# Later hybrid units and the memory stage of a two-block model: order of splits, copies and PSUM banks

## The chip, the cores and the metric

The kernel runs on one core of one Trainium2 chip, in one launch. The metric is the device time in microseconds of one execution. The core has a matrix engine (TensorE, "PE" in the profile, its weight loads "PEld"), a vector engine (VectorE, DVE), a scalar engine (ScalarE, ACT), GpSimd (POOL), and a queue engine (SyncE, SP) that here only issues DMAs.

## The reference, cut to what matters

256 tokens of width 1024 go through two models, each of two layers. A layer of the first model is a gated feed-forward part, a hybrid mixer, cross attention to 256 memory tokens, and a second feed-forward part. The change touches the last two thirds of the hybrid mixer and the cross attention, in both layers.

```python
for l in range(2):
    x = x + 0.5 * rms_norm(swiglu(rms_norm(x, g1), ...), p1)
    y = hybrid_mixer(rms_norm(x, g2), w_in[l], ...)       # attention with window and selection, + retention, then @ w_out
    x = x + rms_norm(y, p2)
    y = memory_xattn(rms_norm(x, g3), rms_norm(mem, gm), wq[l], wk[l], wv[l], wo[l])
    x = x + rms_norm(y, p3)
    x = x + 0.5 * rms_norm(swiglu(rms_norm(x, g4), ...), p4)

def memory_xattn(h, m, wq, wk, wv, wo):                   # 4 heads of 256
    q, k, v = h @ wq, m @ wk, m @ wv
    p = softmax(einsum('bthd,bmhd->bhtm', q, k) / 16)
    return einsum('bhtm,bmhd->bthd', p, v) @ wo
```

## The kernel before, in words

Everything stays on the chip; only weights are streamed. Twelve stages follow one another (`STAGES`): feed-forward, hybrid, memory, feed-forward for layer 0, the same for layer 1 (its hybrid stage begins 651.5 us after that of layer 0), then four stages of the second model. Each of the five engines has its own program, written out by hand in the order in which it runs; engines meet only at semaphores. `q.wait_ge(*act.at("memory", l, 7))` waits until ACT has done the instruction of that name. An engine runs its list in order, so whatever stands behind a wait waits too.

**Splits.** A product in full precision is made of three in a rounded format: each weight item of 128 x 2048 is split into a high part (ACT copies `raw` to `whi`, or to `mhi`) and a low part (DVE subtracts, giving `wlo` or `mlo`), in two halves of 128 x 1024. `take(s, tag, c, ahead)` brings both engines' splits up to that item plus `ahead` items. A split waits for the item's DMA (four `raw` buffers, loaded in order by SP when the item four places earlier is split) and for the last use of the home that it writes. In the second part of the hybrid stage three homes rotate. PE waits for the low part (`weights(i)`).

**Hybrid units.** `HUNITS` are eight units u = 0..7, four heads each; units 0 to 3 belong to the first 128 tokens (m = 0, one key block), units 4 to 7 to the second 128 (m = 1, two key blocks). For a unit, PE makes scores (256 columns of f32 for m = 1), DVE adds the bias and takes the maximum (`head(u)`), ACT makes the exponentials (`exps`), PE turns them (block k = 0 into bank 0, k = 1 into bank 1), ACT copies block 0 and, for m = 1, DVE copies block 1 to `hPT` (both named `h_pt`), PE multiplies with the values (`h_values`, bank 2), DVE scales them (`value`, with `weight` for the factors) and POOL adds them.

Between these, PE does work of the next stage, which needs nothing of the units: sixteen **memory pieces** p = 0..15, two in each unit. Pieces 0 to 7 make one tile of the memory keys each, pieces 8 to 15 the memory values, two pieces for one output. All of them write PSUM bank 3, and ACT copies bank 3 away (`memory_piece` in ACT's program); the next piece that starts an output waits for that copy. In unit u the order on PE is: scores(u+1), piece 2u, turns(u), piece 2u+1, values(u). On ACT: copy of piece 2u, h_pt(u), exps(u+1), copy of piece 2u+1, the split of `HSPLIT[u]` (wk2, wk3, wv0, wv1, wv2, wv3, w_out0, w_out1). On DVE: head(u+1), value(u-1), weight(u), h_pt(u) for m = 1, then the same split. `blocks`, `halves` and `fin` turn and split finished parts of the mixer's output for `w_out`: the retention part in unit 2, the first tokens' attention part in units 4 and 5.

**Memory stage.** After the queries (`wq`, heads 2 and 3 directly, 0 and 1 from the rows `QN`), PE makes for each head c scores, turns and outs, and then multiplies with `wo` (items wo0 and wo1, with more of the heads' work beside them, `beside_0` and `beside_1`, and then wo2 and wo3). DVE's `scores(c)` takes the maximum, waits for ACT's exponentials and scales them. DVE also scales two of the queries (`query(2, 2)`, `query(3, 3)`). PE before the change, from the second tile of wq3 on: scores(1), turn(0), scores(2), outs(0), turn(1), scores(3), wo0, outs(1), turn(2), turn(3), wo1, outs(2), outs(3), wo2 with wo3.

The matmul instruction of all products is L1653, that of all turns L1658; ACT's instruction is L690; DVE's are L1093 (two tensors), L1097 (tensor and scalars), L1101 (tensor, scalar, tensor), L1105 (copy), L1109 (maximum or sum).

Of the kernel before, what the change touches and what calls it, by code (L numbers as in the profile page):

```python
# [262 lines left out]
def build(nc, A, out):  # L263
    ctx = ExitStack()
    with ctx:
# [418 lines left out]
        def scalar(e):  # L684
# [154 lines left out]
            def memory_piece(s, p):  # L839
                l = STAGES[s][1]  # L840
                if p < 8:
                    q.wait_ge(*pe.at("memory", l, p))
                    if p >= 4:
                        q.wait_ge(*dve.at("ret_x", l, 1))
                    put(mkT[:, p * 256:(p + 1) * 256], PS[:, 3, 0:256], ACT.Copy, ("memory", l, p))
                    return
# [13 lines left out]
            def hybrid(s):  # L860
# [69 lines left out]
                for u, (m, g, br) in enumerate(HUNITS):  # L930
                    memory_piece(s, 2 * u)
                    q.wait_ge(*pe.at("h_turned", l, u, 0))
                    put(hPT[u % 2][:, 0:512], PS[:, 0, :], ACT.Copy, ("h_pt", l, u))
                    if u < 7:
                        exps("h", l, u + 1, 128 * (HUNITS[u + 1][0] + 1), hP, 0.125)
                    else:
                        take(s, *HSPLIT[u], 0)
# [6 lines left out]
                    if u == 5:  # L944
                        halves(s + 0.5, 0, 0, 0)
                    if u < 7:
# [12 lines left out]
            def memory(s):  # L959
# [29 lines left out]
                scores(0)  # L989
                scores(1)  # L990
                turned(0)
                scores(2)
                outs(0)
                turned(1)
                scores(3)

                def beside_0():
                    outs(1)
# [88 lines left out]
        def vector(e):  # L1087
# [235 lines left out]
            def hybrid(s):  # L1323
# [134 lines left out]
                head(0)  # L1458
                q.wait_ge(*pe.at("ret_out", l))
# [10 lines left out]
                for u, (m, g, br) in enumerate(HUNITS):  # L1470
                    if u < 7:
                        head(u + 1)
                    if u:
# [13 lines left out]
                    if m:  # L1487
                        q.wait_ge(*pe.at("h_turned", l, u, 1))
                        cp(hPT[u % 2][:, 512:1024], PS[:, 1, :], ("h_pt", l, u))
# [3 lines left out]
                    if u == 4:  # L1493
                        fin(s, l, 0)
                    if u == 5:
# [16 lines left out]
            def memory(s):  # L1512
                l = STAGES[s][1]

                def scores(c):
# [3 lines left out]
                    ts(nb[:, o:o + 2], mx[:, o:o + 2], -0.0625, None, ALU.mult, ALU.bypass, ("ms_max", l, c))  # L1519
                    q.wait_ge(*act.at("ms_exp", l, c, 1))  # L1520
# [16 lines left out]
                take(s, "wq", 3)  # L1537
                query(3, 3)
                scores(0)
                scores(1)  # L1540
                scores(2)
                outs(0)
                scores(3)
                take(s, "wo", 0)
                outs(1)
# [103 lines left out]
        def tensor(e):  # L1649
# [236 lines left out]
            def memory_piece(s, p):  # L1886
                l = STAGES[s][1]
                if p < 8:
# [3 lines left out]
                    if p:  # L1892
                        q.wait_ge(*act.at("memory", l, p - 1))
                    up_tile(hi, lo, f, 3, 0, mhv, mlv, ("memory", l, p), *([("used", i)] if f else []))
# [12 lines left out]
            def hybrid(s):  # L1907
# [134 lines left out]
                for u, (m, g, br) in enumerate(HUNITS):  # L2042
# [7 lines left out]
                    for k in range(m + 1):  # L2050
# [6 lines left out]
                        if u == 6 and k == 0:  # L2057
                            q.wait_ge(*dve.at("a", s + 0.5, 0, 0))
                        if u == 4 and k == 1:
                            q.wait_ge(*dve.at("a", s + 0.5, 1, 1))  # L2060
# [263 lines left out]
```

## Time and profile before

| | us |
|---|---|
| median of 3 runs | 1903.04 |
| lowest and highest of them | 1902.19, 1905.67 |
| the profiled execution's own time | 1902.21 |
| its span, first to last instruction | 1900.4 |
| PE busy | 1858.0 (98%) |
| DVE, ACT, POOL busy | 1317.2, 1042.3, 215.4 |
| granted TensorE clock over the span | 0.994 |

The profile is of one execution. Times in it are counted from the first instruction. A row of the timeline shows when a run of like instructions started and how long it lasted, and in brackets how long the engine had been idle before it and whose instruction ended that wait. The matmuls overlap in the pipe, so what a piece of PE's work costs is read from the starts of neighbouring rows rather than from their lengths. The granted clock is 1.00 where TensorE ran at 2.4 GHz and 0.50 where it ran at 1.2 GHz. All rows below are of layer 0 unless their group says otherwise.

### The profile page before, as it was taken

The numbers are of one execution on the slowest core, as the hardware profiler recorded it, in microseconds if no ns is written. First come the engines' busy times: TensorE is split into PE (matmuls) and PEld (weight loads), VectorE is DVE, ScalarE is ACT, GpSimd is POOL, SyncE is SP. The second block draws the span as 40 slices with busy tenths as digits, with TensorE's granted clock in tenths as the row PEclk, the third lists the DMA queues.
The fourth block names the chain that finished last, engine by engine and source line by source line (L and its number), as shares of the span: only waits on it lengthen the run. The fifth ranks groups of instructions, "written<-read, shape, count | busy, mean of one in ns | idle before, by whom it ended". The sixth has DMA issues, their size and how long they took to land.

```text
span 1900.4 us, 27884 instructions
## 1 busy us (share of the span) xinstructions
PE 1858.0 (98%) x10911; PEld 1617.2 (85%) x10911; DVE 1317.2 (69%) x1734; ACT 1042.3 (55%) x1503; POOL 215.4 (11%) x264
## 2 busy tenths in 40 slices
PE   6999999999999999999999999999999999999998
PEld 6888899788888888888997978888888888888887
DVE  5776758675766676667577667667787667787665
ACT  5555545555555555555465555555666445665453
POOL 1010102010100011001020101000301110301110
PEclk9999999999999999999999999999999999999999
DMA  8585654244565556766333626654636555635552
GB/s 297 184 298 190 165 179 134 89 159 163 173 217 182 180 189 216 268 169 214 121 129 111 204 96 213 201 185 158 211 104 221 179 199 164 219 111 195 193 188 79
DMA packets 229971, 339.46 MB, mean 179 GB/s; under 512 B 22278, under 2 KB 178064, under 8 KB 229840
## 3 DMA queue, kind: packets, MB, share of 16 engines
q1 hardware_dynamic: 221968, 307.91, 49.2%
q0 software_dynamic: 7872, 29.78, 4.8%
q8 instruction: 85, 1.39, 0.3%
q14 instruction: 46, 0.38, 0.1%
HBM read 336.62 MB, written 1.05 MB: 178 GB/s over the span
## 4 chain that ended last, share of the span: by engine, by line
PE 85%; DVE 11%; ACT 2%; issue 1%; DMA 1%; DVEq 0%; SPq 0%; ACTq 0%
PE ps L1653 82%; DVE wlo L1093 3%; PE ps L1658 3%; DVE xn L1093 2%; DVE region L1101 1%; ACT region L690 1%; DVE xs L1101 1%; DVE ahl L1093 1%; DVE mlo L1093 1%; DVE sm L1109 1%; ACT ahl L690 1%; DMA raw<-ffn_w_gate 1%; ACT whi L690 1%; DVE hlo L1093 0%; DVE region L1093 0%
## 5 line engine op out<-in xcount | busy, mean ns | idle before, releaser
L1093 DVE TENSOR_TENSOR wlo<-raw,whi 128x1024 fp32r<-128x1024 f32 (+2 forms) x458 | 561.8, 1227 | 184.8 <-ACT whi L690 150.2
L690 ACT ACTIVATE whi<-raw 128x1024 fp32r<-128x1024 f32 (+2 forms) x458 | 482.5, 1054 | 64.8 <-PE ps L1653 14.9
L1653 PE MATMUL ps<-ahl,whi 128*128 128x512 f32 (+1 forms) x1920 | 433.4, 353 | 0.3
L1653 PEld LDWEIGHTS ps<-ahl,whi 128*128 128x128 f32 x1920 | 331.2, 190 | 43.2 <-DVE hlo L1093 0.9
L690 ACT ACTIVATE region<-ps 128x512 f32<-128x512 f32 (+2 forms) x260 | 150.1, 577 | 326.6 <-PE ps L1653 248.8
L1653 PE MATMUL ps<-whi,ahl 128*128 128x512 f32 (+2 forms) x1120 | 303.6, 349 | 8.8 <-DVE ahl L1093 8.5
L1653 PE MATMUL ps<-ahl,wlo 128*128 128x256 f32 x1568 | 269.1, 282 | 0.0
L1653 PEld LDWEIGHTS ps<-ahl,wlo 128*128 128x128 f32 x1568 | 233.3, 191 | 11.9
L1653 PEld LDWEIGHTS ps<-whi,ahl 128*128 128x128 f32 x1120 | 198.0, 191 | 36.1 <-DVE ahl L1093 12.0
L1093 DVE TENSOR_TENSOR mlo<-raw,mhi 128x1024 fp32r<-128x1024 f32 x130 | 160.9, 1238 | 48.0 <-ACT mhi L690 38.0
L1653 PE MATMUL ps<-wlo,ahl 128*128 128x512 f32 (+2 forms) x560 | 191.6, 342 | 0.0
L1653 PE MATMUL ps<-whi,hhi 128*128 128x512 f32 x472 | 185.6, 393 | 1.1 <-DVE hlo L1093 1.1
L1653 PE MATMUL ps<-wlo,hhi 128*128 128x512 f32 x472 | 184.3, 391 | 0.0
L1653 PE MATMUL ps<-whi,hlo 128*128 128x512 f32 x472 | 183.7, 389 | 0.0
L531 POOL TENSOR_TENSOR hlo<-region,hhi 128x512 fp32r<-128x512 f32 x62 | 81.0, 1306 | 799.7 <-ACT hhi L690 799.7
L1653 PE MATMUL ps<-ahl,mhi 128*128 128x512 f32 (+1 forms) x640 | 144.5, 354 | 0.1
L1653 PE MATMUL ps<-region 128*128 128x64 f32 (+5 forms) x928 | 137.1, 335 | 7.2 <-DVE region L1105 7.1
L690 ACT ACTIVATE mhi<-raw 128x1024 fp32r<-128x1024 f32 x130 | 137.5, 1058 | 11.1 <-PE ps L1653 2.8
L1093 DVE TENSOR_TENSOR region<-region,ps 128x512 f32<-128x512 f32 x102 | 70.2, 688 | 95.4 <-ACT region L690 88.9
L1653 PEld LDWEIGHTS ps<-region 128*128 128x128 f32 (+2 forms) x928 | 113.2, 183 | 26.9 <-ACT region L690 9.7
L690 ACT ACTIVATE hhi<-region 128x512 fp32r<-128x512 f32 x68 | 43.0, 632 | 156.8 <-DVE region L1101 83.4
L1653 PEld LDWEIGHTS ps<-ahl,mhi 128*128 128x128 f32 x640 | 110.8, 190 | 14.6 <-DVE hlo L1093 0.3
(166 smaller groups left out, 2385.0 us busy)
## 6 DMA issues: line engine op xcount, KB each, us to landing
raw<-w_ff SPq DMA_DIRECT2D x64, 1024.0 KB, 5.4
raw<-ffn_w_gate SPq DMA_DIRECT2D x44, 1024.0 KB, 5.3
raw<-ffn_w_up SPq DMA_DIRECT2D x44, 1024.0 KB, 5.5
raw<-ffn_w_down SPq DMA_DIRECT2D x44, 1024.0 KB, 4.9
raw<-w_in SPq DMA_DIRECT2D x38, 1024.0 KB, 5.7
raw<-w_out SPq DMA_DIRECT2D x16, 1024.0 KB, 4.9
raw<-xa_wk SPq DMA_DIRECT2D x8, 1024.0 KB, 5.2
raw<-xa_wv SPq DMA_DIRECT2D x8, 1024.0 KB, 5.0
```

Source lines behind the costliest of these rows:

```text
L531: e.tensor_tensor(o, a, b, op).then_inc(*pool.did(*names))
L690: e.activation(o, i, f, **kw).then_inc(*act.did(*names))
L1093: e.tensor_tensor(o, a, b, op).then_inc(*dve.did(*names))
L1101: e.scalar_tensor_tensor(o, a, s, b, op0, op1).then_inc(*dve.did(*names))
L1109: e.tensor_reduce(o, a, AX.X, op).then_inc(*dve.did(*names))
L1653: m = e.matmul(o, l, r, start=start, stop=stop)
L1658: m = e.transpose(o, i, CS[0:k, 0:k])
```

## The change

It reorders four programs in the hybrid and memory stages and moves four tiles of each hybrid stage to another PSUM bank. No product is added or removed.

- ACT, units 3 to 6: the split of `HSPLIT[u]` stands ahead of exps(u+1); before, it stood at the unit's end. Unit 7 stays as it was.
- DVE, units 4 to 7: the copy h_pt(u) stands ahead of value(u-1) and weight(u). DVE also splits the first half of wk0 right after head(0).
- Memory pieces 1, 3, 5 and 7 write bank 1, and PE waits for the copy of piece p-2. In unit 2, `blocks` of the retention part stand behind values(2) and wait for the copy of piece 5.
- `fin(0)` moves on DVE from unit 4 to unit 5, and `blocks` and `halves` of the first tokens from unit 5 to unit 6 on PE, ACT and DVE.
- Memory stage: DVE's `scores(c)` is cut into `maximum(c)` and `normal(c)`; maximum(0) and normal(0) stand ahead of query(3). ACT's turned(0) stands ahead of exps(1), turned(1) ahead of exps(2), and outs(1) ahead of exps(3). PE's outs(1) stands ahead of wo0.

```diff
@@ -842,7 +842,7 @@
...
                         q.wait_ge(*dve.at("ret_x", l, 1))
-                    put(mkT[:, p * 256:(p + 1) * 256], PS[:, 3, 0:256], ACT.Copy, ("memory", l, p))
+                    put(mkT[:, p * 256:(p + 1) * 256], PS[:, (3, 1)[p % 2], 0:256], ACT.Copy, ("memory", l, p))
                     return
...
@@ -931,19 +931,19 @@
...
                     put(hPT[u % 2][:, 0:512], PS[:, 0, :], ACT.Copy, ("h_pt", l, u))
+                    if u >= 3:
+                        take(s, *HSPLIT[u], 0)
                     if u < 7:
                         exps("h", l, u + 1, 128 * (HUNITS[u + 1][0] + 1), hP, 0.125)
-                    else:
-                        take(s, *HSPLIT[u], 0)
                     memory_piece(s, 2 * u + 1)
...
                         fin(s, l, 0)
-                    if u == 5:
+                    if u == 6:
                         halves(s + 0.5, 0, 0, 0)
-                    if u < 7:
+                    if u < 3:
                         take(s, *HSPLIT[u], 0)
...
@@ -987,15 +987,15 @@
...
                 scores(0)
+                turned(0)
                 scores(1)
-                turned(0)
-                scores(2)
                 outs(0)
                 turned(1)
+                scores(2)
+                outs(1)
                 scores(3)
...
                 def beside_0():
-                    outs(1)
                     turned(2)
...
@@ -1456,6 +1456,7 @@
...
                 head(0)
+                split_to(number[s, "wk", 0], halves=1)
                 q.wait_ge(*pe.at("ret_out", l))
...
@@ -1470,6 +1471,9 @@
...
                         head(u + 1)
+                    if m:
+                        q.wait_ge(*pe.at("h_turned", l, u, 1))
+                        cp(hPT[u % 2][:, 512:1024], PS[:, 1, :], ("h_pt", l, u))
                     if u:
...
@@ -1484,15 +1488,12 @@
...
                     weight(u)
-                    if m:
-                        q.wait_ge(*pe.at("h_turned", l, u, 1))
-                        cp(hPT[u % 2][:, 512:1024], PS[:, 1, :], ("h_pt", l, u))
                     if u == 2:
...
                             halves(s + 0.5, h, 1, h)
-                    if u == 4:
+                    if u == 5:
                         fin(s, l, 0)
-                    if u == 5:
+                    if u == 6:
                         halves(s + 0.5, 0, 0, 0)
...
@@ -1512,11 +1513,14 @@
...
 
-                def scores(c):
+                def maximum(c):
                     o = 2 * (c % 2)
...
                     ts(nb[:, o:o + 2], mx[:, o:o + 2], -0.0625, None, ALU.mult, ALU.bypass, ("ms_max", l, c))
+
+                def normal(c):
+                    o = 2 * (c % 2)
                     q.wait_ge(*act.at("ms_exp", l, c, 1))
...
@@ -1535,14 +1539,18 @@
...
                 take(s, "wq", 3)
+                maximum(0)
+                normal(0)
                 query(3, 3)
-                scores(0)
-                scores(1)
-                scores(2)
+                maximum(1)
+                normal(1)
+                maximum(2)
                 outs(0)
-                scores(3)
+                normal(2)
+                maximum(3)
+                outs(1)
+                normal(3)
                 take(s, "wo", 0)
-                outs(1)
                 take(s, "wo", 1)
...
@@ -1889,9 +1897,11 @@
...
                     hi, lo = weights(i)
-                    if p:
-                        q.wait_ge(*act.at("memory", l, p - 1))
-                    up_tile(hi, lo, f, 3, 0, mhv, mlv, ("memory", l, p), *([("used", i)] if f else []))
+                    if p >= 2:
+                        q.wait_ge(*act.at("memory", l, p - 2))
+                    elif p:
+                        q.wait_ge(*dve.at("g_r", l, 1))
+                    up_tile(hi, lo, f, (3, 1)[f], 0, mhv, mlv, ("memory", l, p), *([("used", i)] if f else []))
                     return
...
@@ -2054,19 +2064,15 @@
...
                             q.wait_ge(*dve.at("h_pt", l, u - 1))
-                        if u == 6 and k == 0:
+                        if u == 7 and k == 0:
                             q.wait_ge(*dve.at("a", s + 0.5, 0, 0))
                         if u == 4 and k == 1:
-                            q.wait_ge(*dve.at("a", s + 0.5, 1, 1))
+                            q.wait_ge(*act.at("memory", l, 7))
                         for i in range(4):
...
                     q.wait_ge(*act.at("h_pt", l, u))
-                    if u == 2:
-                        for h in range(2):
-                            q.wait_ge(*dve.at("ret_x", l, h))
-                            blocks(s + 0.5, h, 1, h)
                     if m:
...
@@ -2076,7 +2082,12 @@
...
                                *([("h_values", l, u)] if (i, k) == (3, m) else []))
-                    if u == 5:
+                    if u == 2:
+                        q.wait_ge(*act.at("memory", l, 5))
+                        for h in range(2):
+                            q.wait_ge(*dve.at("ret_x", l, h))
+                            blocks(s + 0.5, h, 1, h)
+                    if u == 6:
                         q.wait_ge(*dve.at("fin", l, 0))
...
@@ -2139,9 +2150,9 @@
...
                 scores(3)
+                outs(1)
 
                 def beside_0():
-                    outs(1)
                     turn_scores(2)
...
```

## Rows read from the trace of the kernel before

**Rows 1.** The page: busy time, share of the span and instructions of each engine.
```profile
PE 1858.0 (98%) x10911; PEld 1617.2 (85%) x10911; DVE 1317.2 (69%) x1734; ACT 1042.3 (55%) x1503; POOL 215.4 (11%) x264
```

**Rows 2.** Windows: length, busy of five engines, clock, DMA.
```profile
355.87:362.69 6.82, 6.82 (x17) 4.94 (x17) 5.74 (x8) 1.99 (x2) 0.55 (x1) 0.50 0.26 62
444.62:448.02 3.40, 3.40 (x11) 2.77 (x10) 1.42 (x5) 1.73 (x5) 0.00 (x0) 0.50 0.00 0
1007.82:1014.63 6.81, 6.81 (x17) 4.89 (x16) 6.15 (x9) 1.53 (x2) 0.14 (x1) 0.50 0.30 88
1096.57:1099.96 3.39, 3.39 (x10) 2.64 (x9) 1.41 (x5) 1.73 (x5) 0.00 (x0) 0.50 0.02 5
```

**Rows 3.** Timeline of PE, units 4 to 7.
```profile
345.11 0.50 PE L1653 MATMUL ps<-whi,mhi 128*128 128x512 f32 x1
...
347.98 1.03 PE L1658 MATMUL ps<-cs,region 128*128 128x128 f32 x8
...
348.77 0.47 PE L1653 MATMUL ps<-whi,mhi 128*128 128x512 f32 x1
...
353.90 5.65 PE L1653 MATMUL ps<-region 128*128 128x64 f32 x24 [2.13 <-DVE region L1105]
...
367.47 1.89 PE L1653 MATMUL ps<-region 128*128 128x64 f32 x16
...
369.73 1.99 PE L1653 MATMUL ps<-region 64*128 64x256 f32 x8
...
371.65 0.50 PE L1653 MATMUL ps<-whi,mhi 128*128 128x512 f32 x1
...
379.74 1.97 PE L1653 MATMUL ps<-region 128*128 128x64 f32 x16 [1.44 <-DVE region L1105]
```

**Rows 4.** Timeline of DVE, units 3 and 4.
```profile
345.71 2.56 DVE L1093 TENSOR_TENSOR wlo<-raw,whi 128x1024 fp32r<-128x1024 f32 x2 [2.83 <-ACT whi L690]
...
350.19 1.22 DVE L1109 TENSOR_REDUCE sm<-region 128x4 f32<-128x1024 f32 x1
...
353.07 0.69 DVE L1105 COPY region<-ps 128x512 f32<-128x512 f32 x1
```

**Rows 5.** Timeline of ACT, units 3 to 5.
```profile
341.55 0.51 ACT L690 ACTIVATE region<-region,sm 128x256 f32<-128x256 f32 x1 [1.85 <-DVE sm L1097]
...
344.62 2.15 ACT L690 ACTIVATE whi<-raw 128x1024 fp32r<-128x1024 f32 x2
...
351.65 0.51 ACT L690 ACTIVATE region<-region,sm 128x256 f32<-128x256 f32 x1 [2.44 <-DVE sm L1097]
...
354.24 0.60 ACT L690 ACTIVATE region<-ps 128x512 f32<-128x512 f32 x1
```

**Rows 6.** Timeline of PEld, PE and ACT, units 0 and 2.
```profile
311.53 0.19 PEld L1653 LDWEIGHTS ps<-mhi,whi 128*128 128x128 f32 x1 [0.27 <-ACT region L690]
...
331.73 1.04 PE L1658 MATMUL ps<-cs,xn 128*128 128x128 f32 x8
...
332.60 2.92 PE L1653 MATMUL ps<-region 128*128 128x64 f32 x16
...
332.67 0.38 ACT L690 ACTIVATE region<-ps 128x256 f32<-128x256 f32 x1
```

**Rows 7.** Timeline of PE, memory stage.
```profile
440.21 1.89 PE L1653 MATMUL ps<-region 128*128 128x256 f32 x8
...
444.26 0.82 PE L1658 MATMUL ps<-cs,region 128*128 128x128 f32 x4 [2.16 <-DVE region L1097]
...
452.28 0.50 PE L1653 MATMUL ps<-whi,ahl 128*128 128x512 f32 x1
...
457.83 1.89 PE L1653 MATMUL ps<-region 128*128 128x256 f32 x8
...
461.14 0.50 PE L1653 MATMUL ps<-whi,ahl 128*128 128x512 f32 x1 [0.54 <-DVE ahl L1093]
```

**Rows 8.** Timeline of DVE, memory stage.
```profile
435.21 2.55 DVE L1093 TENSOR_TENSOR wlo<-raw,whi 128x1024 fp32r<-128x1024 f32 x2
```

## The prediction

> **What bounds the kernel now.** I read the page's first part first: PE is busy 98% of the span, DVE 69% and ACT 55% [rows 1]. So only time in which PE waits, or in which its clock is low, can be won, and there are some 42 us of the first kind in the whole span. The waits of PE alone, and then the granted clock by windows, show that the stretch that the change touches holds a large part of both. In units 4 and 6 PE stands idle 2.13 and 1.44 us, and what ends the wait is a DVE copy, h_pt(u) [rows 3]. In the memory stage it stands 2.16 us before turn(0), ended by a DVE scaling, and 0.54 us before wo1 [rows 7]. Counted from where PE's previous work was through, the four gaps are 2.3, 1.6, 2.3 and 0.7 us. Right after the first and the third the granted clock is 0.50, for 6.82 and 3.40 us, with PE busy throughout; it is 0.50 at the same places of layer 1, for 6.81 and 3.39 us [rows 2]. Work at half the clock takes twice its time, so these cost 3.4 and 1.7 us in a layer. The sum in each layer: 2.3 + 3.4 + 1.6 = 7.3 us in the units and 2.3 + 1.7 + 0.7 = 4.7 us in the memory stage, 24 us in all. Nothing else in reach is as large.
>
> **Why PE waits in unit 4.** The chain is read backwards through three timelines. The copy h_pt(4) starts at 353.07 and ends at 353.76, and PE goes on at 353.90 [rows 3, 4]. DVE was not idle before it: head(5) ran until 351.61 (its maximum at 350.19, and a small operation), then value(3) and weight(4), 1.4 us. Head(5) began only at 348.37, behind the split of wv1, which started at 345.71 after 2.83 us of waiting for ACT [rows 4]. ACT began that split at 344.62, since it had exps(4) ahead of it [rows 5]. PE had its second piece through at 348.77 + 2.87 = 351.6 [rows 3].
>
> **ACT's split ahead of the exponentials, DVE's copy ahead of the values (units 3 to 6).** Take unit 3. ACT is free at 339.7 and waits 1.85 us for head(4), until 341.55 [rows 5]; the split (2.15 us [rows 5]) goes into that gap and is through at 341.9. The exponentials (2.5 us, from 351.65 to the copy at 354.24 in the like unit [rows 5]) start 0.3 us later than before and end at 344.4. DVE then finds the high half ready when weight(3) is done, at 342.9, and splits until 345.5, not 348.27. Head(5) can start at 345.5, as its scores end near 344.9, and takes 3.24 us: until 348.75. The turns end at 348.77 [rows 3], so the copy h_pt(4) runs from 349.0 to 349.7 and value(3) until 350.2. PE needs both at 351.6. The stall is gone with 1.4 us to spare.
>
> What is late next is ACT. Its order in unit u is now copy, split, exps(u+1), copy of piece 2u+1, and PE's next output waits for the last. From the start of the turns ACT needs 0.6 us to its copy, 0.7 for it, 2.15 for the split, 2.5 for the exponentials and 0.7 for the last copy: about 6.7. PE has, from the same point, the turns 0.8, a piece 2.87, the values 1.73 (367.47 to 369.73, less 0.53 for the four turns that stand there in between) and the scores 1.92 (369.73 to 371.65 [rows 3]): 7.3. Margin 0.5 us, in units 4 and 5. In unit 6 there are no scores, since unit 7 is the last; there are now four turns of the first tokens instead, 0.5 us. PE has 5.9 us, ACT needs 6.7: **a new stall of about 0.9 us** before piece 14. Its ends: 0, if ACT starts as much earlier as PE does, and 1.5. The moved fin(0) and blocks cost only this; PE did the same turns in unit 5 before. On POOL the root of fin(0) now stands ahead of the sum of unit 4 and waits for DVE's later fin_var(0); value(6), which needs that sum, comes some 15 us behind. SP's loads follow the low splits, which come earlier, so the loads come earlier too; DMA is used 26% there [rows 2].
>
> The balance in the units from 4 on: 7.3 - 0.9 = **6.4 us**.
>
> **Two banks and the moved blocks (units 0 to 3).** Before, each odd piece waited for ACT's copy of the piece before it: PE's weight load was idle 0.27 us at piece 1 [rows 6], and the same shows in four units. With bank 1 that goes, 4 x 0.2 us. The first half of wk0's split, moved into DVE's wait for the retention product, brings piece 0 0.3 us forward, at the price of 0.6 us on the retention part, for which PE does not wait. Together up to 1.1 us before unit 2 ends. But the blocks of unit 2 must now wait for the copy of piece 5, and that stands on ACT behind exps(3): it ended at 333.05, and at best 332.5 after the change [rows 6]. PE did the blocks at 331.73, before the values (332.60) [rows 6]; now it would be through with the values at 331.3 and stand about 1.2 us. The scores of unit 4 then start when they did before. Here I take **0 us** net, with the ends +0.9 (PE's gain survives) and -0.5 (the halves behind the blocks push head(4) back).
>
> **Memory stage.** Before, DVE took query(3) at 440.41, then the maximum of head 0, whose scores had been there since 437.3. Now maximum(0) follows the split that ends at 437.77 [rows 8], ACT makes the exponentials (1.16 us) in a time in which it was idle, and normal(0) is through at 440.9; query(3), 0.7 us, at 441.6. PE ends scores(1) at 440.21 + 1.73 = 441.94 [rows 7] and goes straight on. The rest in PE's new order from 440.21: scores(1), scores(2), outs(0), scores(3), outs(1), five times 1.73; two times four turns, 0.87; wo0, 5.55 (452.28 to 457.83 [rows 7]); eight turns, 0.87. That is 15.9 us, and wo1 starts at 456.2 and not at 461.14. Step by step no wait ends late: normal(1) at 445.4 against 445.8 is the closest, 0.4 us. So **4.8 us** (4.9 by this sum, 4.7 by the stalls). Ends: 3.1, if the 1.7 us of low clock stay, and 5.0.
>
> **The sum.** (6.4 + 0 + 4.8) x 2 layers = 22.4 us. The profiled execution took 1902.21 us with a span of 1900.4; that would become 1879.8 and 1878.0. It lies 0.8 us under the median of the runs, 1903.04, and the forecast is made against this: **1880.6 us**. The other stages are bound by PE and should only shift.
>
> **Rivals.**
>
> *The clock falls do not go with the stalls.* Then only 2.3 + 1.6 - 0.9 and 2.3 + 0.7 us come back in a layer, 6.0 x 2, and the kernel takes 1891 us. For it: the clock stayed at 1.2 GHz while PE worked without a gap on the values and scores of unit 4, and the stall of unit 6 (1.44 us) was followed by none. Against it: both falls of a layer begin within two us of the end of a stall of over 2 us, at the same places of both layers, and units 5 and 6, with the same kind of work but no such stall, ran at 2.4 GHz. The three runs lie within 3.5 us, so four falls that come and go are not likely. The Trainium skill, "TensorE: Matmul & The Clock Gate", section "The HAM clock gate (the 'warmup' mystery)", says that the clock's change does not keep step with the kernel, so the same kernel can meet it at other places from run to run; by that, part of the 10.2 us need not have been in every run of before. The rows show the same four places twice over. Chance 0.10.
>
> *The clock falls at a new place.* The stall of 1.2 us in unit 2 lies between small values and turns, and that of 0.9 us in unit 6 behind values and turns. If the clock falls at one of them in each layer, for 3.4 or 6.8 us, it costs 1.7 or 3.4 us each: 1884 to 1887.4. Chance 0.15.
>
> *ACT becomes the bound.* If its copies come 1 us later than the margin of 0.5 allows, at pieces 10, 12 and 14 in both layers, 6 us are lost: 1886.6. It would show as PE waiting for ACT at L690 at these pieces. Chance 0.09.
>
> *Slower.* The same queue, but with the split itself waiting. It now stands ahead of everything that PE needs of ACT, so a late raw tile or a home still in use would hold up the exponentials and the copies. Four splits in each layer; to lose the 22.4 us and 3.8 more, each must wait 26.2 / 8 + 0.5 = 3.8 us. Against it: the home of a split in unit u was last used by piece 2u at the latest, before the turns that ACT waits for, and the tiles landed long before; ACT's splits show no DMA wait in these units. Chance 0.03: 1907 us or more.
>
> *It does not do what it says.* The copy might not be what PE waited for: PE also waits for h_out(u-1), which DVE had made at 352.13, and that too moves forward. If units 4 and 6 kept their stalls for a cause that I have not seen, the memory stage alone would give 1903.04 - 9.6 = 1893.4. Chance 0.02.
>
> **Chances and range.** The forecast has 0.61, with its own range of 1876.5 to 1883.5: below, the new stalls of units 2 and 6 are absent (-1.8 and -1.8) and the medians differ; above, the half us in unit 2 and one stall of 1.5 us. With the new falls and the ACT case the range is 1876.5 to 1887.5, which leaves out 0.15 and some of the tails. Faster by over 0.2% (3.8 us, about what a measurement of this kernel can tell from no change): 0.95; within 0.2%: 0.02; slower: 0.03.
>
> **What would show it.** Right: in PE's timeline values(4) and values(6) follow pieces 9 and 13 without a gap; no window of 0.50 clock behind them; turn(0) follows scores(1); wo1 starts 16 us after scores(1). A wait of about 1.2 us for ACT ahead of the blocks of unit 2 and of 0.9 us ahead of piece 14. The low clock windows of 20.4 us in these stages are gone. Wrong: new windows at 0.50, or pieces 10 and 12 waiting for L690.

## The result, and the profile after

The changed kernel takes 1881.62 us (median of 4 runs, 1880.94 to 1882.39) against 1904.36 us (1902.19 to 1906.17) for the kernel before on the same chip: 0.9881 of the time, 95% interval 0.9864 to 0.9898, or 22.7 us less. The forecast was 1880.6. The profiled execution took 1881.63 us with a span of 1879.6.

The page's first part, to be held against [rows 1]:

```profile
PE 1844.7 (98%) x10911; PEld 1610.6 (86%) x10911; DVE 1314.6 (70%) x1734; ACT 1042.5 (55%) x1503; POOL 216.5 (12%) x264
```

PE is busy 13 us less for the same 10911 matmuls. Shorter waits don't do that; the clock does: half of the 20.4 us of [rows 2] is 10.2 us of it. The other 3 stand in the same stages: between the same matmuls of layer 0, PE's busy time in units 0 to 3 falls from 41.08 to 40.19 us and in the memory stage from 18.17 to 15.79, of which the clock is 1.7; so some of the time that PE loses is counted as busy (turns(0) to values(0) took 3.61 us and takes 3.32, with no idle time in the rows of either). By windows (length, busy time of five engines, granted clock, DMA) the units and the memory stage of both layers now stand at 1.00; [rows 2] had four stretches at 0.50:

```profile
345.00:391.00 46.00, 45.16 (x247) 38.00 (x246) 34.38 (x53) 28.30 (x54) 4.78 (x7) 1.00 0.35 119
435.27:465.00 29.73, 29.73 (x144) 25.19 (x143) 19.16 (x30) 17.29 (x30) 0.00 (x0) 1.00 0.39 133
985.00:1032.00 47.00, 46.16 (x251) 38.87 (x250) 35.40 (x53) 29.28 (x56) 5.42 (x8) 1.00 0.36 122
1073.00:1103.00 30.00, 30.00 (x155) 25.83 (x154) 18.53 (x33) 17.49 (x32) 0.00 (x0) 1.00 0.45 152
```

PE's timeline of the units, layer 0 (start, length, what, and in brackets the idle time before it and who ended it). It answers to [rows 3] and [rows 6]; this execution reached the units 1.2 us later than the one of before, since its first 25 us took that much longer.

```profile
333.70 1.09 PE L1666 MATMUL ps<-cs,xn 128*128 128x128 f32 x8 [0.96 <-ACT region L690]
...
343.44 3.00 PE L1661 MATMUL ps<-region 128*128 128x64 f32 x16 [0.35 <-DVE region L1093]
...
349.25 1.03 PE L1666 MATMUL ps<-cs,region 128*128 128x128 f32 x8
...
352.89 3.81 PE L1661 MATMUL ps<-region 128*128 128x64 f32 x24
...
373.37 1.89 PE L1661 MATMUL ps<-region 128*128 128x64 f32 x16
375.10 0.61 PE L1666 MATMUL ps<-cs,xn 128*128 128x128 f32 x4
...
376.54 0.50 PE L1661 MATMUL ps<-whi,mhi 128*128 128x512 f32 x1 [0.84 <-ACT region L690]
...
383.04 1.89 PE L1661 MATMUL ps<-region 128*128 128x64 f32 x16
```

Values(4) at 352.89 and values(6) at 373.37 follow their pieces without a gap; before they had 2.13 and 1.44 us. Values(4) and the scores behind it take 3.81 us, against 5.65, of which all but the first 2 us were at half the clock. Two waits for ACT are new: 0.96 us ahead of the blocks of unit 2 (333.70) and 0.84 ahead of piece 14 (376.54). From turns(4) to values(7) it is 33.79 us, where it was 387.98 - 347.98 = 40.00. Values(7) in the kernel before:

```profile
387.98 1.89 PE L1653 MATMUL ps<-region 128*128 128x64 f32 x16
```

DVE and ACT in units 3 and 4, against [rows 4] and [rows 5]:

```profile
344.22 2.55 DVE L1093 TENSOR_TENSOR wlo<-raw,whi 128x1024 fp32r<-128x1024 f32 x2
...
348.70 1.22 DVE L1109 TENSOR_REDUCE sm<-region 128x4 f32<-128x1024 f32 x1
...
350.32 0.69 DVE L1105 COPY region<-ps 128x512 f32<-128x512 f32 x1 [0.20 <-PE ps L1666]
351.12 0.42 DVE L1093 TENSOR_TENSOR region<-ps,sm 128x256 f32<-128x256 f32 x1
```

```profile
340.98 2.15 ACT L690 ACTIVATE whi<-raw 128x1024 fp32r<-128x1024 f32 x2
343.22 0.51 ACT L690 ACTIVATE region<-region,sm 128x256 f32<-128x256 f32 x1
...
350.57 2.15 ACT L690 ACTIVATE whi<-raw 128x1024 fp32r<-128x1024 f32 x2
...
355.41 0.60 ACT L690 ACTIVATE region<-ps 128x512 f32<-128x512 f32 x1
```

ACT splits wv1 at 340.98, in what was idle time; DVE has its half of the split through at 346.77, the maximum of head(5) starts at 348.70, the copy h_pt(4) ends at 351.01 and value(3) at 351.54, 1.35 us before PE goes on to values(4). ACT's copy behind the exponentials of unit 4 ends at 356.01; PE starts piece 10 at 356.63. These 0.6 us are the margin now.

PE in the memory stage, against [rows 7]:

```profile
435.27 1.89 PE L1661 MATMUL ps<-region 128*128 128x256 f32 x8
437.00 0.60 PE L1666 MATMUL ps<-cs,region 128*128 128x128 f32 x4
437.44 3.62 PE L1661 MATMUL ps<-region 128*128 128x256 f32 x16
...
451.06 0.48 PE L1661 MATMUL ps<-whi,ahl 128*128 128x512 f32 x1
```

Scores(1) starts at 435.27, turn(0) right behind it, wo1 at 451.06: 15.79 us, where it was 461.14 - 440.21 = 20.93. DVE had maximum(0) done before scores(1) began:

```profile
432.95 0.69 DVE L1109 TENSOR_REDUCE sm<-ps 128x2 f32<-128x512 f32 x1
...
436.12 0.69 DVE L1093 TENSOR_TENSOR region<-ps,region 128x512 f32<-128x512 f32 x1
```

**Where the time went.** Between the same matmuls of both traces, layer 0's units and memory stage are 11.3 us shorter and layer 1's 10.9. The first 25 us are 1.2 us longer, where the two programs are the same and two executions of the kernel before differ by 0.75 too (e11); the rest is the same to 0.3 us. That is 20.8 of span, between these two executions; the medians differ by 22.7.

### The profile page after: what moved, and what is told of

Same layout as the page of the kernel before. It is cut to its first block, busy times and chain, and to the rows that moved or that the text cites. A ratio compares the mean times of both kernels' runs of the same rounds, so it can differ in the third digit from the quotient of the medians.

```text
span 1879.6 us, 27894 instructions
## 1 busy us (share of the span) xinstructions
PE 1844.7 (98%) x10911; PEld 1610.6 (86%) x10911; DVE 1314.6 (70%) x1734; ACT 1042.5 (55%) x1503; POOL 216.5 (12%) x264
## 4 chain that ended last, share of the span: by engine, by line
PE 85%; DVE 11%; ACT 3%; issue 1%; DMA 1%; DVEq 0%; SPq 0%; ACTq 0%
PE ps L1661 82%; DVE wlo L1093 3%; PE ps L1666 3%; DVE xn L1093 2%; DVE region L1101 1%; ACT region L690 1%; DVE xs L1101 1%; DVE mlo L1093 1%; DVE ahl L1093 1%; ACT whi L690 1%; DMA raw<-ffn_w_gate 1%; ACT ahl L690 0%; DVE sm L1109 0%; DVE hlo L1093 0%; DVE region L1585 0%
## 5 line engine op out<-in xcount | busy, mean ns | idle before, releaser
L1661 PEld LDWEIGHTS ps<-whi,ahl 128*128 128x128 f32 x1120 | 197.9, 191 | 34.6 <-DVE ahl L1093 10.2
L1661 PE MATMUL ps<-region 128*128 128x64 f32 (+5 forms) x928 | 130.0, 326 | 0.7 <-DVE region L1093 0.7
L1661 PEld LDWEIGHTS ps<-region 128*128 128x128 f32 (+2 forms) x928 | 109.4, 179 | 17.4 <-issue 3.6
```

The lines of the kernel that those rows point to most:

```text
L1661: m = e.matmul(o, l, r, start=start, stop=stop)
```

## Experiments

Every kernel is the changed one with one edit, but for e6, which has two, and e11, which is the kernel before. The kernel before ran beside them: 1903.89 us in the first series (e1 to e4), 1905.07 in the second (e5 to e8), 1904.04 in the third. The changed kernel did not, so a difference to its 1881.6 of about 1 us is no more than the series differ among themselves; such a difference rests on the traces. My theory going in: the early split on ACT takes the waits of PE away, and a fall of the clock comes with a wait of over 2 us.

### ACT's split back behind the exponentials (e1)

```diff
@@ ACT, units @@
-                    if u >= 3:
-                        take(s, *HSPLIT[u], 0)
                     if u < 7:
                         exps("h", l, u + 1, ...)
+                    else:
+                        take(s, *HSPLIT[u], 0)
...
-                    if u < 3:
+                    if u < 7:
                         take(s, *HSPLIT[u], 0)
```

> The changed kernel, with ACT's split of HSPLIT[u] in units 3 to 6 back behind exps(u+1). DVE's copy stays ahead of value and weight. My theory: the split of wv1 comes back to where it holds up head(5), so PE waits about 1.25 us in unit 4 and 0.9 us in unit 5 for DVE, and the 0.85 us wait for piece 14 goes: net +1.4 us in each layer, 1884.4 us, and no low clock, since no stall passes 2 us. Rival 1, the clock falls with this kind of work and any stall in unit 4: two windows of 0.50 clock come back, +3.4 us in each layer more, 1891. Rival 2, the copy's new place alone cures the stall: 1881.6 or less.

Measured: 1888.3 us (1884.94, 1887.98, 1888.62, 1889.16), 0.9906 of before [0.9876, 0.9937]. PE's values(4) and (5) of layer 0, then values(4) of layer 1, and the stretch at low clock behind this last one:

```profile
354.25 3.89 PE L1661 MATMUL ps<-region 128*128 128x64 f32 x24 [1.28 <-DVE region L1093]
...
365.37 3.89 PE L1661 MATMUL ps<-region 128*128 128x64 f32 x24 [0.64 <-DVE region L1093]
...
995.76 6.12 PE L1661 MATMUL ps<-region 128*128 128x64 f32 x24 [1.30 <-DVE region L1093]
```

```profile
997.12:1007.36 10.24, 10.24 (x28) 7.65 (x28) 5.52 (x8) 3.22 (x5) 0.00 (x0) 0.50 0.29 102
```

Waits come in units 4 and 5, that of piece 14 goes, and the 1.44 us that the kernel before had in unit 6 doesn't come back: +1.3 us in layer 0 from turns(4) to values(7) (35.08 for 33.79), with no fall. Layer 1 has the same wait in unit 4 (1.30) and behind it a stretch at 0.50 of 10.24 us; at this clock PE doesn't wait in unit 5, and it takes 38.94. So, with all other parts in place, the split is worth 1.3 us in a layer in plain waits and up to 3.9 us more in clock: 6.7 us of the whole by the medians, where the units' share of the gain is 12.4. The rest comes by the other parts even without it. It also takes my theory down: the fall follows a wait of 1.30 us, in one layer and not in the other. The fastest run, at a mean clock of 1.0, lies at the sum without a fall, the other three (0.997 to 0.998) 3 to 4 us above it.

### DVE's copy back behind the values (e2)

```diff
@@ DVE, units @@
-                    if m:
-                        q.wait_ge(*pe.at("h_turned", l, u, 1))
-                        cp(hPT[u % 2][:, 512:1024], PS[:, 1, :], ("h_pt", l, u))
                     if u:
                         value(u - 1)
...
                     weight(u)
+                    if m:
+                        q.wait_ge(*pe.at("h_turned", l, u, 1))
+                        cp(hPT[u % 2][:, 512:1024], PS[:, 1, :], ("h_pt", l, u))
```

> The changed kernel, with DVE's copy h_pt(u) back behind value(u-1) and weight(u). My theory: with the split early, the copy of unit 4 would end at 352.2 us where PE needs it at 352.9, that of unit 6 0.4 us ahead of need: no new wait, 1881.6 us within 0.5. Rival, the copy's place is what cures units 4 and 6: PE waits again about 1.2 us in each, +2.4 us in each layer, 1886.4.

Measured: 1881.86 us (1881.54 to 1883.15), 0.9878 of before [0.9854, 0.9901]: no change. The copy starts 1.27 us later than in the changed kernel, counted from turns(4) (349.54 us here, 349.25 there), and still ends before PE comes:

```profile
351.88 0.69 DVE L1105 COPY region<-ps 128x512 f32<-128x512 f32 x1
```

```profile
353.18 3.81 PE L1661 MATMUL ps<-region 128*128 128x64 f32 x24
```

With the split early, the copy's place earns nothing. It may work as a reserve: with the split late (e1) PE waits 1.28 us in unit 4 where the kernel before, with both late, waited 2.13. Unit 6's wait of 1.44 us comes back in neither; whether the copy or the later fin(0) took it away in e1 was not tried.

### One bank for the memory pieces (e3)

```diff
@@ PE, memory pieces 0 to 7 (ACT's copy reads bank 3 to match) @@
-                    if p >= 2:
-                        q.wait_ge(*act.at("memory", l, p - 2))
-                    elif p:
-                        q.wait_ge(*dve.at("g_r", l, 1))
-                    up_tile(hi, lo, f, (3, 1)[f], 0, ...)
+                    if p:
+                        q.wait_ge(*act.at("memory", l, p - 1))
+                    up_tile(hi, lo, f, 3, 0, ...)
@@ PE, unit 2: blocks ahead of the values again, with no wait for piece 5 @@
```

> The changed kernel, with all memory pieces in bank 3 and the blocks of unit 2 ahead of the values, as before the change. My theory: the 0.96 us wait ahead of the blocks goes, four waits of 0.2 us at the odd pieces come back, and DVE's chain to values(3) sets the pace in any case: between -0.6 and 0 us over both layers, 1881.0 to 1881.6. Rival, the second bank earns what its waits cost (0.2 us at 4 pieces, 2 layers): 1883.3.

Measured: 1880.84 us (1880.08 to 1881.01), 0.987 of before [0.9846, 0.9894], 0.8 us under the changed kernel and 0.2 under my range. The blocks of unit 2 no longer wait:

```profile
332.89 1.04 PE L1666 MATMUL ps<-cs,xn 128*128 128x128 f32 x8
333.76 2.92 PE L1661 MATMUL ps<-region 128*128 128x64 f32 x16
```

Nor does values(3), which I had expected DVE's chain to hold up in any case. Up to turns(4) the layer is 0.45 us shorter. The two waits (0.96 and 0.35) were 1.3 us, so the second bank earns some 0.9 us and the moved blocks lose 1.3: this part of the change costs 0.4 us in a layer. The two were not put back one by one.

### The memory stage back (e4)

```diff
@@ DVE (scores(c) = maximum(c) and normal(c) together; ACT and PE orders to match) @@
-                maximum(0)
-                normal(0)
                 query(3, 3)
-                maximum(1)
-                normal(1)
-                maximum(2)
+                scores(0)
+                scores(1)
+                scores(2)
                 outs(0)
...
@@ PE @@
                 scores(3)
-                outs(1)
...
```

> The changed kernel, with the memory stage as before the change. My theory: the stall of 2.16 us before turn(0), the one before wo1 and the low clock after the first come back in both layers: 2 x 5.1 = 10.3 us, 1891.9 us, with a window of 0.50 clock after each stall. Rival, the falls of the clock were a matter of that run and not of the stall: only the stalls come back, 2 x 3.4 = 6.9 us, 1888.5, with no such windows.

Measured: 1891.07 us (1890.87 to 1891.45), 0.9925 of before [0.9901, 0.9949], 9.4 us above the changed kernel. Turn(0) waits again, and in layer 0 the clock falls behind it:

```profile
439.30 1.12 PE L1659 MATMUL ps<-cs,region 128*128 128x128 f32 x4 [2.16 <-DVE region L1097]
...
456.15 0.50 PE L1654 MATMUL ps<-whi,ahl 128*128 128x512 f32 x1 [0.54 <-DVE ahl L1093]
```

```profile
439.29:442.70 3.41, 3.40 (x10) 2.94 (x11) 1.73 (x5) 1.73 (x5) 0.00 (x0) 0.50 0.00 0
```

In layer 1 the clock stays at 1.00, and a wait stands there that the slow PE of layer 0 doesn't have:

```profile
1087.51 1.99 PE L1654 MATMUL ps<-region 128*128 128x256 f32 x8 [0.49 <-ACT region L690]
```

The two layers lose 5.1 and 4.2 us against the changed kernel: the fall of 3.41 us costs 0.9 net, not 1.7, mostly because at full clock PE has to wait for ACT instead (outs(0) starts 2.38 us behind scores(2), which takes 1.73). The stage's part of the gain is 4.7 us a layer.

### Unit 6 alone back (e5), and with one bank (e6)

```diff
@@ ACT, units (e5) @@
-                    if u >= 3:
+                    if u >= 3 and u != 6:
                         take(s, *HSPLIT[u], 0)
...
-                    if u < 3:
+                    if u < 3 or u == 6:
                         take(s, *HSPLIT[u], 0)
```

> In unit 6 alone ScalarE's split of w_out goes back behind the exponentials of unit 7; all else is the changed kernel. Theory: the 0.84 us that TensorE waits ahead of piece 14 for ScalarE's copy of the turned half (375.7 us in the changed kernel) comes only from the 0.69 us split and the copy queued behind the exponentials; without it the wait goes and nothing takes its place, so 1881.6 - 2 x 0.85 = 1879.9 us (1879.3 to 1880.7). Rival: piece 15's halves of w_out then come late in turn, because this split is what they wait for: a new wait of 0.6 to 1.4 us ahead of piece 15 and no gain or a loss, 1881.5 to 1883 us.

> The changed kernel with all memory pieces in one bank and the blocks of unit 2 back ahead of the values (as in e3), and with ScalarE's split of unit 6 back behind the exponentials. Theory: the two savings lie in different places (wait of unit 2 and of values(3) near 333 and 343 us, wait ahead of piece 14 near 376 us) and add: 1880.8 (e3) - 1.7 = 1879.1 us (1878.5 to 1880.0), under the changed kernel. Rival: with the pieces in one bank, TensorE's pieces 13 and 14 wait for ScalarE's copy of the piece ahead of them, so that the wait ahead of piece 14 stays whatever the split does: 1880.5 to 1881.5 us.

e5: 1879.79 us (1878.75 to 1880.21), 0.9862 of before [0.9845, 0.9879]. Its turns of the first tokens and piece 14 of layer 0:

```profile
375.23 0.61 PE L1666 MATMUL ps<-cs,xn 128*128 128x128 f32 x4
375.59 0.47 PE L1661 MATMUL ps<-whi,mhi 128*128 128x512 f32 x1
```

The wait is gone, as foreseen, and nothing waits in its place. From turns(4) to values(7) both layers take 32.7 us for 33.8: counted from the starts of rows, the wait cost 1.1 us, more than the 0.84 of its row. e6, with e3's edit on top: 1878.27 us (1878.07 to 1878.47), 0.9855 [0.9838, 0.9872]. The two savings add, so its rival is out. It came 0.8 us under my number. In e6's trace e3's edit brings 0.4 to 0.5 us a layer up to turns(4), and the split of unit 6 brings 1.1 us a layer from there to values(7), where I had 0.85: that is 0.5 of the 0.8 us. e6 is the fastest of all: 3.3 us under the changed kernel, though the two ran in different series.

### The final normalisation back (e7)

```diff
@@ DVE (ACT's and PE's part one unit earlier to match) @@
-                    if u == 5:
+                    if u == 4:
                         fin(s, l, 0)
-                    if u == 6:
+                    if u == 5:
                         halves(s + 0.5, 0, 0, 0)
```

> The final normalisation fin(0) back in unit 4 on VectorE, and its blocks and halves back in unit 5, as before; everything else as in the changed kernel. Theory: VectorE then waits in unit 4 for ScalarE's square and holds the head of unit 6 up, which gives TensorE a wait of 2.3 to 2.8 us in unit 5 where the changed kernel has none, less some 0.4 us that the wait ahead of piece 14 loses: +2.3 us a layer, 1886.2 us if no fall of the clock comes with it and up to 1893 us with a fall in each layer. Rival: VectorE has room enough in unit 4 once its copy stands ahead of the values, so that fin's place is neutral: 1881.2 to 1882.4 us.

Measured: 1897.13 us (1892.63 to 1899.23), 0.9952 of before [0.9935, 0.9969], 15.5 us above the changed kernel and above my upper end. PE, and the stretches behind the first wait of each layer:

```profile
365.51 3.22 PE L1661 MATMUL ps<-region 128*128 128x64 f32 x16 [2.40 <-ACT region L690]
...
384.27 0.50 PE L1661 MATMUL ps<-whi,mhi 128*128 128x512 f32 x1 [1.28 <-ACT region L690]
```

```profile
365.98:376.22 10.24, 10.24 (x33) 8.12 (x33) 5.87 (x9) 1.83 (x5) 0.19 (x1) 0.50 0.17 45
1014.51:1024.75 10.24, 10.24 (x31) 7.93 (x31) 6.22 (x9) 1.42 (x4) 0.00 (x0) 0.50 0.20 78
```

The wait in unit 5 came as worked out, 2.40 us. Its row names ACT, but ACT's copy had ended at 360.54; what PE needed last was DVE's copy and value(4), through at 365.36. Two things were too small in my sum: the wait of 0.84 us ahead of a piece didn't shrink, but stands at 1.28, and the falls last 10.24 us instead of 6.8. For a layer 2.40 + (1.28 - 0.84) + 5.12 = 7.96 us; from turns(4) to values(7) the trace shows 41.69 - 33.79 = 7.90. The early split and the late fin(0) belong together: with fin(0) in unit 4, DVE stands 4.47 us for ACT's square, which is queued behind split and exponentials, and head(6) comes late.

### A wait of chosen length (e8, e9, e10)

```diff
@@ DVE, units: n = 5 (e8), 3 (e9), 4 (e10) @@
                     if m:
                         q.wait_ge(*pe.at("h_turned", l, u, 1))
+                        for _ in range(n if u == 4 else 0):
+                            cp(hPT[u % 2][:, 512:1024], PS[:, 1, :])
                         cp(hPT[u % 2][:, 512:1024], PS[:, 1, :], ("h_pt", l, u))
```

> The changed kernel with five more copies of the turned half (0.69 us each, the same operands) on VectorE in unit 4, ahead of the one that TensorE waits for; the result is unchanged. It puts a wait of about 2.3 us (1.6 to 2.5) on TensorE in unit 4, in the place where the kernel before had its 2.1 us. First theory (the clock falls with every wait over 2 us in this stretch): a stretch at 0.50 in both layers, costing 3.4 us each as in the kernel before: 1881.6 + 2 x (2.3 + 3.4) = 1893.0 us, all runs alike. Second theory (a wait in this stretch brings a fall in some layers and executions and not in others): the runs spread between 1886.2 us (no fall) and 1893.0 us (two), in steps of 3 to 4 us. Third (falls have nothing to do with waits): 1886.2 us and no low stretch.

> As e8_five_copies with three more copies in place of five: each copy took 0.72 us there, so the wait in unit 4 should be 2.27 - 2 x 0.72 = 0.83 us, one in each layer. First theory (whether a fall of the clock comes goes by the length of the wait; the changed kernel itself has waits of 0.8 to 1.0 us and no fall): no low stretch in the two units' places and 1881.6 + 2 x 0.83 = 1883.3 us (1882.6 to 1884.2). Second theory (the place decides, and any wait in unit 4 brings a fall): stretches at 0.50 as in e8, 1883.3 + 2 x 4 = 1891 us.

> As e8_five_copies with four more copies in place of five: a wait of 2.27 - 0.72 = 1.55 us in unit 4 in each layer. First theory (the length of the wait decides, and 1.3 us, e1's, is where falls come in some executions and not in others): the sum without a fall is 1881.6 + 2 x 1.55 = 1884.7 us; e8's falls cost (1894.6 - 1881.6 - 4.5) / 2 = 4.2 us a layer, so the runs spread over 1884.7 to 1893.2 us, most of them with at least one fall, median 1889 to 1893. Second theory (falls need a wait of over 2 us): 1884.7 us (1884.2 to 1885.5) in all runs.

PE's values(4) of layer 0 in e9, e10 and e8, in this order:

```profile
354.50 3.89 PE L1663 MATMUL ps<-region 128*128 128x64 f32 x24 [0.82 <-DVE region L1093]
```

```profile
354.87 5.58 PE L1663 MATMUL ps<-region 128*128 128x64 f32 x24 [1.54 <-DVE region L1093]
```

```profile
355.47 5.76 PE L1663 MATMUL ps<-region 128*128 128x64 f32 x24 [2.27 <-ACT region L690]
```

The stretches at low clock of e10, then of e8, in both layers; e9 has none in these stages:

```profile
356.91:363.74 6.83, 6.83 (x16) 4.95 (x17) 4.30 (x7) 0.19 (x2) 0.00 (x0) 0.50 0.48 155
1002.03:1008.86 6.83, 6.83 (x16) 4.92 (x17) 4.22 (x8) 0.25 (x2) 0.00 (x0) 0.50 0.41 154
```

```profile
357.21:364.04 6.83, 6.83 (x18) 4.93 (x17) 4.13 (x7) 0.00 (x0) 0.00 (x0) 0.50 0.45 155
1002.33:1012.57 10.24, 10.24 (x30) 7.94 (x30) 5.48 (x8) 0.68 (x2) 0.00 (x0) 0.50 0.29 104
```

| wait in unit 4 | kernel | runs, us | without a fall it would be |
|---|---|---|---|
| 0.82 | e9 | 1884.11, 1884.30, 1884.42, 1887.28 | 1883.3 |
| 1.3 (and 0.64 in unit 5 of layer 0) | e1 | 1884.94, 1887.98, 1888.62, 1889.16 | 1884.4 |
| 1.54 | e10 | 1885.90, 1892.12, 1892.79, 1893.65 | 1884.7 |
| 2.27 | e8 | 1894.11, 1894.43, 1894.85, 1895.30 | 1886.2 |

(Medians, and ratios to before: e9 1884.36, 0.99 [0.9884, 0.9917]; e10 1892.46, 0.9931 [0.9913, 0.9948]; e8 1894.64, 0.9941 [0.992, 0.9961].) The last column is the changed kernel's 1881.6 and twice the wait (for e1, the number on record). Each kernel has one profiled execution; of its other runs only the time and the mean clock are known (e10: 0.999 in the lowest, 0.995 in the upper three; e8: 0.995, 0.994 in all).

The waits are those of the copies less the room that there was: 3, 4 and 5 times 0.72 us, less 1.35, are 0.81, 1.53 and 2.25. (In e8's row too the engine named is not the one: ACT's copy ended at 350.64, DVE's value(3) at 355.31.) At 0.82 us the runs lie 1 us above the sum, once 4. The waits cost more than their rows say: in both layers e9 takes 34.88 us from turns(4) to values(7) for 33.79, which is 1.09 for a wait of 0.82. Over both layers that is 0.5 of the 1 us above the sum; 0.6 more stands in the first 25 us of this execution. At 1.54 one run of four looks by time and clock as without a fall and three as with two, which the profiled one of them shows. At 2.27 all four look like the profiled one, with two falls, whose length is not the same in both layers: 6.83 and 10.24 us. From turns(4) to values(7), e8's layers take 5.7 and 7.3 us more than the changed kernel's: 2.27 + 3.41 and 2.27 + 5.12. So in unit 4, as far as four runs of each kernel show, the fall is the surer the longer the wait, and nothing at 2 us divides the cases; and the wait alone doesn't decide, since in e4 2.16 us ahead of turn(0) brought a fall in layer 0 and none in layer 1. E10's first theory holds, its median inside the range; of e9's the first holds in three runs of four, with a median 0.2 us above the range. Of e8's expectations the first came nearest in the time (1893.0), but its reason, a limit at 2 us, is refuted by e1 and e10.

### The kernel before once more (e11)

> The kernel before unchanged, profiled a second time, for the places and lengths of its stretches at 0.50. If the waits fix the falls: the same four places (6.8 us from about 356 and 1008 us, 3.4 us from about 445 and 1097 us). If each fall is a matter of chance once the wait is there: another number or other lengths (3.4, 6.8 or 10.2 us), with the time following at half of the difference in low microseconds.

One execution, 1903.04 us. Its stretches at low clock:

```profile
356.80:363.63 6.83, 6.83 (x17) 4.86 (x17) 5.95 (x8) 1.79 (x2) 0.40 (x1) 0.50 0.26 82
445.55:448.96 3.41, 3.41 (x11) 2.70 (x10) 1.23 (x5) 1.73 (x5) 0.00 (x0) 0.50 0.01 2
1008.75:1015.58 6.83, 6.83 (x17) 4.87 (x17) 6.31 (x10) 1.34 (x2) 0.00 (x0) 0.50 0.34 112
1097.49:1100.90 3.41, 3.41 (x9) 2.68 (x9) 1.73 (x5) 1.63 (x6) 0.00 (x0) 0.50 0.00 0
```

The same four places with the same lengths as [rows 2]. In two profiles the waits of 2.1 us brought a fall eight times out of eight; the upper runs of the kernel before (up to 1912.6 us at a mean clock of 0.990, where the profiled ones have 0.994) are as if falls were longer or more, but none of them was profiled. So the repeat speaks for falls that are fixed by the waits in this kernel, while e4 and e10 show that they need not be.

## Why the prediction was right

**What bounds it.** Right: four waits in a layer and four stretches at half the clock in both, and the rest only shifted, to 0.3 us. Between the same matmuls the two stages of both layers are 22.2 us shorter, where the sum had 22.4. The time itself came 1.0 us above the forecast: that started from 1903.04, the median of three runs, and with a fourth the kernel before stands at 1904.36.

**Units 4 to 6, 6.4 us a layer.** Measured 6.2 in both. Each step of the chain is there: the split in ACT's idle time, head(5) earlier, copy and value(3) ready with 1.35 us to spare, where I had 1.4. The new wait ahead of piece 14 was put at 0.9; its row says 0.84, and without it (e5) the layer is 1.1 us shorter. That is the 0.2 us that the sum lacks: 7.3 - 1.1 = 6.2. E5 also shows that the split on ACT in unit 6 alone makes it. The margin of 0.5 us at piece 10 is 0.6.

**Banks and blocks, 0 net.** From scores(1) to piece 8 it was 38.56 us and is 38.62. PE gains 1.2 us up to the end of piece 5 (24.00 us from scores(1) for 25.18) and loses it in the two waits behind, as argued. The wait of 1.2 us is 0.96. I had not seen that values(3) would wait another 0.35. That the term is near nought hid a loss: e3 and e6 show that with one bank and the blocks in their old place 0.45 us a layer come back. What wk0's early split earns was not tried alone.

**Memory stage, 4.8 us.** The trace shows 5.1 in layer 0 and 4.9 in layer 1, e4 4.7 as a mean of both. From scores(1) to wo1 it is 15.8 us, as worked out (15.9).

**Credit for the parts.** I gave the copy on DVE and the split on ACT one sum. e1 and e2 divide it in part: given the split, the copy earns nothing, but without the split (e1) units 4 to 6 are still shorter than before, by 4.9 us in layer 0 and 1.0 in layer 1, where the clock fell. The split alone, with the copy and fin(0) in their old places, was not tried, so how much each would bring by itself stays open. And I costed the move of fin(0) as the price of a new wait only; e7 shows that it is needed, since with the split early, leaving it in unit 4 costs 7.8 us a layer.

**The clock.** The forecast took all of the 10.2 us of low clock as going with the waits, and it was right: none is left there. The rival that they do not go with the waits (1891) fell, with e8 and e10, where a wait made of copies alone brings them. But I argued from stalls of "over 2 us", on four cases and on unit 6's 1.44 us without a fall; e1 (1.30) and e10 (1.54) show falls below that. So my second rival, a fall behind the new waits of 0.96 and 0.84 us, may have been weighed too lightly at 0.15: e9, with an added wait of 0.82, had one run of four at 3 us above the others and at a lower mean clock (0.998); it was not the profiled one. In the four runs of the changed kernel (clock 0.999 to 1.0) it didn't happen. The Trainium skill ("TensorE: Matmul & The Clock Gate", section "The HAM clock gate (the 'warmup' mystery)") says of the slow matmuls at a kernel's start that their number varies from run to run. No row here is of the start; e10's runs, 1885.9 to 1893.7 us for one kernel at mean clocks of 0.999 and 0.995, show the like in mid-kernel. ACT never became the bound, and no split waited for its tile.

**Left open.** What besides its length makes a wait bring a fall, and for how long. Unit 6 of the kernel before (1.44 us, no fall in two profiles) and unit 4 of e10 (1.54 us, by time and clock a fall in three runs of four) stand close together and differ in the work around them. But that work can't decide alone: in e1 (1.28 and 1.30 us) and in e4 (2.16 and 2.16) it is the same in both layers, and the clock fell in one of them.

## What to carry to other kernels

Where PE waits, follow the waiting engine's queue backwards past its own work: here the copy was late because of a split two steps ahead of it, which waited for ACT's half of the same split, queued behind exponentials. Moving that half into ACT's idle time was enough for unit 4's wait (e2), and moving the copy brought nothing on top; but parts that cure the same wait can't be added, so a part put back alone shows what it earns beside the others and not what it would earn by itself. A wait of PE can cost more than its length: its row can understate it by 0.25 us (0.84 and 0.82 us cost 1.1), so measure between starts, and up to 5.1 us of lost clock came on top in these stages, and in unit 4 the more surely the longer the wait. And when work moves ahead on one engine, ask in which unit PE has less to do than elsewhere: there (unit 6) the same move costs 1.1 us a layer instead of earning, so make it unit by unit. Work that waits for what now comes later (fin(0) in unit 4) has to move back with it.

## What was not expected of the hardware

A stretch at half the clock lasted 3.41, 6.83 or 10.24 us, and the wait before it doesn't fix which: 2.27 us brought 6.83 in one layer and 10.24 in the other of the same execution (e8). Such a stretch costs half its length only where PE doesn't have to wait for another engine anyway; in e4 3.41 us cost 0.9. And a wait of only 1.3 us was followed by a fall of 10.24 us (e1).
